# Routing stretch reordered, last two experts returned by one-hot products, final norm by rows

## The chip, the cores and the metric

The kernel runs on one core of one Trainium2 chip. The metric is the device time of one execution in microseconds. Five engines run their own instruction streams and meet at semaphores: TensorE (PE), VectorE (DVE), ScalarE (ACT), GpSimd (POOL) and SyncE (SP). POOL, SP and ACT also issue DMAs; those of SP carry the weights.

## The reference

One inference step of a two-layer backbone for 128 context tokens and 256 latent tokens, in float32, width 1024. What matters here is the second half of each layer and the final norm:

```
h2 = rmsnorm(x) * (1 + scale2) + shift2
x  = x + gate2 * moe(h2)            # 16 experts, 2 chosen for each token
...
y_prompt, y_sample = rmsnorm(xp, final_norm_g), rmsnorm(xs, final_norm_g)

def moe(h, ...):
    scores = sigmoid(h @ router_w); ...        # best group of 4, then its best 2 experts
    z = silu(h @ w_gate[e]) * (h @ w_up[e]) * gates[e]
    return sum over e of z @ w_down[e]         # w_gate, w_up: 1024x512, w_down: 512x1024
```

## The kernel before

All 384 tokens are three tiles of 128 rows (NT = 3; tile 0 is the context). The order of every engine's work is written out by hand; there is no scheduler. Each PSUM use is a job with a bank of its own (`place_jobs`), `fill`, `ready`, `release` and `moved` are the semaphore steps around it. A `step` waits until the instruction before it has written its result.

**Weights.** SP loads 2 MB blocks in the order `ISSUE` into six slots (`ring` 0 to 3, `extra` 4 and 5). A block is issued when the block that was in its slot has been read (`block_read`). Blocks are `ada` (modulation), `win`, `wout`, and for each expert gate, up and down. Beside the last products of layer 0, TensorE reads four `ada` blocks of layer 1, `AHEAD[0]`, by `mod_rows` (8 products each, 16 recorded instructions); `mod_turn` then turns their result.

**Routing stretch.** When x of a tile is done, it is normed, turned, modulated (`hidden_tile`), turned back and stored in DRAM as `hidden_rows` (ACT issues that store). `route` gives the logits; VectorE then runs some sixty small steps: scores, the one-hot choices `oh1`, `oh2`, each choice's place in its expert's list (`place6`), and, by a product with the one-hot `inplace`, the lists `lst` of at most 96 rows for each expert (CAP = 96). An expert with more rows than that would get a further round: the overflow table `ovt` holds their number and what they are. With these inputs there are none, and the overflow loop is only jumped over.

**Experts.** POOL gathers the 96 rows of an expert from `hidden_rows` into `xg` (L667), TensorE turns them (L1824) and runs gate, up and down (L1835), ACT and VectorE move the halves out of PSUM; the result lands in one of two buffers `ybuf` (VectorE L1414, L1416 last), and POOL scatters it to `expert_rows` in DRAM (L685), two rows for each token. The weights of expert e+1 land during expert e.

**End of a layer.** All five engines read `ovt` and jump over the overflow loop. POOL waits until every store has landed, reloads both rows of all tokens (L711, three DMAs of 1 MB, one for each tile), and VectorE adds them tile by tile, multiplies by the gate and adds to x (L1453 to L1455, 128x1024 each). ACT sums the squares (L733, L734), VectorE norms the tile (L1008 to L1003 small steps, L1010 the product). In layer 0 the first turns of layer 1 (L1510) follow, which wait for all three tiles. At the end of layer 1 one product with the final gain runs over all tiles (L1460), and SP stores the results.

## Time and profile before

| | |
|---|---|
| time of three runs | 1343.4, 1341.26, 1334.2 us, median 1341.26 |
| the profiled execution | 1344.76 us, its span 1343.1 us |
| TensorE busy | 1170.7 us, 87% of the span |
| VectorE, ScalarE, GpSimd busy | 525.6, 371.5, 249.6 us |
| chain that ended last | TensorE 74%, VectorE 14%, DMA 7% |
| layer 0: experts' products | 387.6 to 660.95 us |
| layer 1: experts' products | 1032.5 to 1305.9 us |

The span is from the first to the last recorded instruction. Within the experts TensorE has hardly a gap; outside them it often waits.

### The profile page before, as it was taken

The numbers are of one execution on the slowest core, as the hardware profiler recorded it, in microseconds if no ns is written. First come the engines' busy times: TensorE is split into PE (matmuls) and PEld (weight loads), VectorE is DVE, ScalarE is ACT, GpSimd is POOL, SyncE is SP. The second block draws the span as 40 slices with busy tenths as digits, with TensorE's granted clock in tenths as the row PEclk, the third lists the DMA queues.
The fourth block names the chain that finished last, engine by engine and source line by source line (L and its number), as shares of the span: only waits on it lengthen the run. The fifth ranks groups of instructions, "written<-read, shape, count | busy, mean of one in ns | idle before, by whom it ended". The sixth has DMA issues, their size and how long they took to land.

```text
span 1343.1 us, 19689 instructions
## 1 busy us (share of the span) xinstructions
PE 1170.7 (87%) x7740; PEld 540.9 (40%) x7740; DVE 525.6 (39%) x1276; ACT 371.5 (28%) x730; POOL 249.6 (19%) x361
## 2 busy tenths in 40 slices
PE   2899899789969999999629989988896999999980
PEld 0555555354423333333225655555443333333320
DVE  1274666733422111111154747575145111111125
ACT  2123344331312222222121424452222222222221
POOL 1221274220020111110020324440202011111000
PEclk9899889789879999999959997996996999999995
DMA  9738321555769999999380312064733999999924
GB/s 364 258 125 124 65 95 67 213 200 226 317 232 379 382 382 389 400 393 377 113 301 0 134 63 83 12 222 167 300 117 149 346 396 390 391 389 384 391 113 161
DMA packets 51488, 322.71 MB, mean 240 GB/s; under 512 B 8329, under 2 KB 8777, under 8 KB 32080
## 3 DMA queue, kind: packets, MB, share of 16 engines
q1 hardware_dynamic: 37552, 286.87, 55.3%
q0 software_dynamic: 12576, 30.03, 8.4%
q10 hardware_dynamic: 1280, 4.72, 0.9%
q8 instruction: 53, 0.87, 0.3%
q14 instruction: 27, 0.22, 0.1%
HBM read 315.53 MB, written 22.73 MB: 252 GB/s over the span
## 4 chain that ended last, share of the span: by engine, by line
PE 74%; DVE 14%; DMA 7%; issue 2%; ACT 2%; SPq 0%; DVEq 0%; POOLq 0%; ACTq 0%
PE ps L1835 38%; PE ps L1476 18%; PE ps L1724 6%; PE ps L1824 3%; DMA ring<-ada_w 3%; DVE attT L1103 3%; DVE dbuf L1082 2%; PE ps L1487 2%; PE ps L1510 2%; PE ps L1647 1%; PE ps L1618 1%; DMA ring<-w_out 1%; DVE small L1208 1%; DVE dbuf L1078 1%; DMA expert_rows<-big,lst 1%
## 5 line engine op out<-in xcount | busy, mean ns | idle before, releaser
L1835 PE MATMUL ps<-ring,dbuf 128*32 128x512 f32 x3072 | 390.2, 598 | 3.0 <-DVE dbuf L1395 1.6
L1835 PE MATMUL ps<-extra,dbuf 128*32 128x512 f32 x1536 | 198.4, 596 | 0.0
L1835 PEld LDWEIGHTS ps<-ring,dbuf 128*32 128x32 f32 x3072 | 108.6, 111 | 212.9 <-issue 207.4
L1476 PE MATMUL ps<-ring,extra 128*128 128x512 f32 (+1 forms) x384 | 149.8, 550 | 0.0
L1476 PE MATMUL ps<-extra,ring 128*128 128x384 f32 (+1 forms) x384 | 127.8, 481 | 7.6 <-ACT extra L763 5.1
L685 POOL DMA_INDIRECT expert_rows<-big,lst x32 | 30.0, 939 | 468.6 <-DVE big L1416 446.5
L1835 PEld LDWEIGHTS ps<-extra,dbuf 128*32 128x32 f32 x1536 | 56.1, 110 | 121.1 <-issue 120.9
L1476 PEld LDWEIGHTS ps<-ring,extra 128*128 128x128 f32 x384 | 74.0, 194 | 69.7 <-issue 66.2
L1476 PEld LDWEIGHTS ps<-extra,ring 128*128 128x128 f32 x384 | 75.7, 207 | 54.8 <-issue 12.7
L1395 DVE COPY dbuf<-ps 128x384 f32<-128x384 f32 x32 | 17.8, 558 | 200.5 <-PE ps L1824 200.4
L1724 PE MATMUL ps<-ring,extra 128*128 128x512 f32 x192 | 87.5, 612 | 7.6 <-DMA ring<-w_out 6.4
L952 ACT ACTIVATE big<-ps 96x512 f32<-96x512 f32 x32 | 19.0, 594 | 219.9 <-issue 163.1
L1487 PE MATMUL ps<-ring,scp 128*32 128x512 f32 x384 | 55.8, 717 | 26.9 <-DMA ring<-ada_w 26.9
L1405 DVE TENSOR_TENSOR big<-big,ps 64x512 f32<-64x512 f32 x32 | 21.7, 679 | 143.1 <-ACT big L961 143.1
L667 POOL DMA_INDIRECT dbuf<-hidden_rows,lst x32 | 31.2, 975 | 173.6 <-DMA hidden_rows<-big 75.8
L1414 DVE COPY big<-ps 64x512 f32<-64x512 f32 x32 | 22.2, 693 | 99.4 <-PE ps L1835 99.4
L1724 PEld LDWEIGHTS ps<-ring,extra 128*128 128x128 f32 x192 | 37.0, 197 | 51.5 <-issue 49.8
L1103 DVE COPY_PREDICATED attT<-mk,ps 128x128 f32<-128x128 uint16 x168 | 50.6, 301 | 15.6 <-PE ps L1647 10.0
L1510 PE MATMUL ps<-const,big 128*128 128x128 f32 x160 | 22.3, 287 | 35.5 <-DVE big L1010 35.5
L789 ACT ACTIVATE big<-ps 128x512 f32<-128x512 f32 (+2 forms) x42 | 21.6, 515 | 103.9 <-PE ps L1476 81.1
L467 POOL TENSOR_TENSOR dbuf<-bbuf 128x128 f32<-128x128 f32 x56 | 24.8, 443 | 132.6 <-PE ps L1647 128.9
L870 ACT ACTIVATE ring<-ps,small 128x384 f32<-128x384 f32 (+1 forms) x56 | 27.3, 488 | 71.8 <-DVE small L1209 71.0
(281 smaller groups left out, 1393.2 us busy)
## 6 DMA issues: line engine op xcount, KB each, us to landing
ring<-moe_w_up SPq DMA_DIRECT2D x30, 2048.0 KB, 14.1
ring<-ada_w SPq DMA_DIRECT2D x24, 2048.0 KB, 8.9
ring<-moe_w_gate SPq DMA_DIRECT2D x24, 2048.0 KB, 14.0
extra<-moe_w_down SPq DMA_DIRECT2D x22, 2048.0 KB, 14.4
ring<-w_in SPq DMA_DIRECT2D x12, 2048.0 KB, 11.6
ring<-moe_w_down SPq DMA_DIRECT2D x10, 2048.0 KB, 18.5
extra<-moe_w_gate SPq DMA_DIRECT2D x8, 2048.0 KB, 14.8
ring<-w_out SPq DMA_DIRECT2D x4, 2048.0 KB, 9.8
```

The costliest lines, as they stand in the source:

```text
L467: step(eng.tensor_tensor(strided(out, n * 2 * P + P + m, [-P, 2], [M, nb], [1, m]), right, ref, ALU.subtract))
L667: pool.indirect_dma_start(xg[0:CAP, e % 2, :], None, hrow, bass.IndirectOffsetOnAxis(lst[0:CAP, e, 0:1], 0), bounds_check=T - 1, oob_is_er ...
L685: pool.indirect_dma_start(yrow, bass.IndirectOffsetOnAxis(lst[0:CAP, e - 1, 1:2], 0), ybuf[0:CAP, (e - 1) % 2, :], None, bounds_check=2 * ...
L870: release(act, act.activation(prob[:, i % 2, mp, 0:nk], p[:, 0:nk], ACT.Exp, scale=scale, bias=nmx[:, i % 2, mp:mp + 1], accum_out=sums[:, ...
L1082: step(dve.tensor_tensor(o_, o_, strided(k0, 0, [HP * T + m, 2], [M, nb], [1, m]), ALU.mult))
L1103: ins = dve.copy_predicated(attT[:, 2 * u + h2, :], mk[:, 4 * g + k, :].bitcast(mybir.dt.uint16), p[:, k * P:(k + 1) * P])
L1476: ins = pe.matmul(out, a, b, start=(n == 0), stop=(n == len(pairs) - 1))
L1487: ins = pe.matmul(ps[c:c + 32, MOD_BANK, :], scp[:, 2 * b + k, :], w[:, 2048 * k + 512 * n:2048 * k + 512 * (n + 1)], start=(b == 0 and k ...
L1510: ins = pe.transpose(p[:, n * P:(n + 1) * P], s, ident)
L1724: ins = pe.matmul(p, hT[:, k, t * P:(t + 1) * P], w[:, k, :], start=(k == WO_ORDER[0]), stop=(k == WO_ORDER[-1]))
L1824: ins = pe.transpose(p[:, n * CAP:(n + 1) * CAP], s, ident[0:CAP, 0:CAP])
L1835: return pe.matmul(p[QT * g:QT * (g + 1), :], a, w, start=start, stop=stop, tile_position=(0, QT * g))
```

## The change

1. **Routing stretch, TensorE.** In layer 0 the four `ada` blocks of layer 1 are read at other places: none right after `route(0)`, the first after the first two products of the logits, the second behind `hidden_back(2)`, the last two together behind the lists.
2. **Routing stretch, VectorE.** The count of the overflow rounds is worked out before the lists (between `posn` and `lst`) and signalled by a semaphore of its own (`s_nov`). Behind the table come eight new steps: `yidx`, an index for each row of `expert_rows` that points out of bounds where the row's expert is 14 or 15 (and its place is under 96), and `late`, the one-hot matrices of those two experts' rows. The modulation of `AHEAD` stands behind them.
3. **Overflow loop in front.** Every engine reads the count and jumps before its first expert. SP holds the fourth expert block (`j == 3`) until the count is known and the first expert's rows have been gathered (`d_g[0]`); the third block goes to slot 5 in both layers.
4. **Last two experts.** Only experts 0 to 13 are scattered. In each layer POOL clears the two reload buffers during expert 4 (L731) and, as soon as the store of expert 13 has landed, fetches the others' rows by six indirect DMAs of 512 KB (L745). So that rows not yet written are finite, `expert_rows` is first filled with x by two DMAs (768 rows of 4 KB) on POOL's queue ahead of the skewed bias table (L627).
5. **The sum.** VectorE sums tile 0's fetched rows before it moves out the last half of expert 15, and tile 1's after; POOL does so for tile 2. TensorE multiplies `late` with `ybuf` (12 products with 512 columns), and `completed` adds the result times the gate to x.
6. **Norms.** They run tile by tile inside the sum; the final one takes the gain in the same instruction, and SP stores each tile by itself.

```diff
@@ SP, in the loop over ISSUE[l]
                     elif kind == "expert":
+                        if j == 3:
+                            overflow_weights(l)
+                            sp.wait_ge(d_g[0], 16 * (NE // 2 * l + 1))
@@ SP, at the end
-            sp.wait_ge(s_y, 1)
-            sp.dma_start(y_prompt[0], xn[:, 0, :]).then_inc(d_y, 16)
-            sp.dma_start(y_sample[0].rearrange("(t p) d -> p t d", p=P), xn[:, 1:3, :]).then_inc(d_y, 16)
+            for t in range(NT):
+                sp.wait_ge(s_y, t + 1)
+                sp.dma_start(y_sample[0, (t - 1) * P:t * P] if t else y_prompt[0], xn[:, t, :]).then_inc(d_y, 16)
@@ POOL
                 if l == 0:
+                    for rows_, src in ((yrow[0:2 * P], x_prompt[0]), (yrow[2 * P:2 * T], x_sample[0])):
+                        pool.dma_start(rows_.rearrange("(p k) d -> p k d", k=2),
+                                       src.unsqueeze(1).broadcast_to([src.shape[0], 2, D])).then_inc(d_init, 16)
                     pool.dma_start(skew, ...)
...
                 for b in range(2):
-                    pool.wait_ge(d_sc[b], 16 * (NE // 2) * (l + 1))
+                    pool.wait_ge(d_sc[b], 16 * ((NE - LATE) // 2) * (l + 1))
+                pool.wait_ge(s_late, l + 1)
                 for t in range(NT):
-                    pool.dma_start(yr[:, t, :, :], yrow[2 * t * P:2 * (t + 1) * P].rearrange("(p k) d -> p k d", k=2)).then_inc(d_yr[t], 16)
+                    for k in range(2):
+                        pool.indirect_dma_start(yr[k][:, t, :], None, yrow, bass.IndirectOffsetOnAxis(yidx[:, NT * k + t:NT * k + t + 1], 0),
+                                                bounds_check=2 * T - 1, oob_is_err=False).then_inc(d_yr[t], 16)
+                pool.wait_ge(d_yr[2], 32 * (l + 1))
+                y = yr[0][:, 2, :]
+                step(pool.tensor_tensor(y, y, yr[1][:, 2, :], ALU.add))
+                step(pool.tensor_tensor(y, y, gate[:, 1, :], ALU.mult))
+                pool.tensor_tensor(x[:, 2, :], x[:, 2, :], y, ALU.add).then_inc(s_sum2, 1)
@@ DVE, after the last expert but one
+                summed(0)
+                expert(NBODY, 0, last=True, next_=False)
+                summed(1)
+                completed(0)
+                completed(1)
+                normalize(2 * l + 2, 0)
+                dve.wait_ge(s_sum2, l + 1)
+                completed(2)
+                normalize(2 * l + 2, 1)
+                normalize(2 * l + 2, 2)
@@ DVE
+                def completed(t):
+                    for b in range(2):
+                        job = ("cm", l, t, b)
+                        p = ready(dve, job)
+                        tmp_ = dbuf[:, b * 512:(b + 1) * 512]
+                        release(dve, dve.tensor_tensor(tmp_, p, gate[:, min(t, 1), b * 512:(b + 1) * 512], ALU.mult), job)
+                        xs = x[:, t, b * 512:(b + 1) * 512]
+                        ins = dve.tensor_tensor(xs, xs, tmp_, ALU.add)
...
@@ PE, after expert 15
+                for t in range(NT):
+                    halves = [begin(pe, ("cm", l, t, b)) for b in range(2)]
+                    for j in range(LATE):
+                        if t == 0:
+                            for kind in ("dn0", "dn1"):
+                                moved(pe, (kind, l), NE - LATE + j)
+                        for b in range(2):
+                            ins = pe.matmul(halves[b], late[0:CAP, j, t, :], ybuf[0:CAP, j, b * 512:(b + 1) * 512], ...)
```

TensorE in the routing stretch of layer 0, before: `L1770` is `route`, `L1487` is `mod_rows`, `L1505` spreads the gates, `L1804` to `L1806` are the places and the last `L1476` the lists.

```order
178 L1770 MATMUL ps<-dbuf,wrt 32x256 x8
179 L1487 MATMUL ps<-ring,scp 32x512 x16
180 L1510 MATMUL ps<-const,big 128x128 x8
181 L1790 MATMUL ps<-const,dbuf 128x16 x2
182 L1487 MATMUL ps<-ring,scp 32x512 x8
183 L1770 MATMUL ps<-dbuf,wrt 32x128 x8
...
186 L1505 MATMUL ps<-bbuf,const 128x512 x4
...
191 L1476 MATMUL ps<-bbuf 96x48 x6
192 L1487 MATMUL ps<-ring,scp 32x512 x8
193 L1497 MATMUL ps<-const,dbuf 128x8 x4
194 L1824 MATMUL ps<-const,dbuf 128x96 x8
```

The same place after (`L1843` is `route`, `L1560` is `mod_rows`, `L1578` spreads the gates).

```order
178 L1843 MATMUL ps<-dbuf,wrt 32x256 x8
179 L1583 MATMUL ps<-const,big 128x128 x8
180 L1861 MATMUL ps<-const,dbuf 128x16 x2
181 L1560 MATMUL ps<-ring,scp 32x512 x8
182 L1843 MATMUL ps<-dbuf,wrt 32x128 x8
...
185 L1560 MATMUL ps<-ring,scp 32x512 x8
186 L1578 MATMUL ps<-bbuf,const 128x512 x4
...
191 L1549 MATMUL ps<-bbuf 96x48 x6
192 L1560 MATMUL ps<-ring,scp 32x512 x16
193 L1570 MATMUL ps<-const,dbuf 128x8 x4
194 L1967 TENSOR_LOAD ovt
...
196 L1968 COMPARE_AND_BRANCH
```

One block instead of three stands ahead of the second `route`, one ahead of the gates, two ahead of `mod_turn`, and the read of the count stands ahead of the first expert's turns.

VectorE between the places and the first expert, after (before, the rows 411 to 417 stood behind the lists, and the rows from 440 on did not exist, save the modulation 446).

```order
410 L1390 TENSOR_TENSOR attT<-ps,const 128x48
411 L1393 COPY attT<-ps 128x16
...
417 L1399 SCALAR_TENSOR_TENSOR attT<-const,attT 128x16
418 L1400 CAST ovt<-attT 1x1
419 L1402 TENSOR_SCALAR lst<-ps 96x16
...
439 L1429 CAST ovt<-attT 1x7
440 L1430 TENSOR_TENSOR attT<-attT 128x6
...
444 L1435 TENSOR_SCALAR attT<-lst 96x2 x3
445 L1436 TENSOR_TENSOR bbuf<-const,attT 96x768
446 L1063 TENSOR_TENSOR modv<-ps,par 128x32
447 L1472 TENSOR_LOAD ovt
...
464 L1447 COPY dbuf<-ps 128x384 x2
```

Eight small steps and one read of the count are added between the lists and row 464, which moves the first expert's turned rows, and eight small ones have left it.

VectorE at the end of layer 0, after: rows 540 and 545 are the last of experts 14 and 15, `L1500` to `L1502` are `summed`, `L1510` and `L1512` `completed`, `L1055` ends a norm.

```order
540 L1468 TENSOR_TENSOR big<-big,ps 64x512
541 L1500 TENSOR_TENSOR big<-big,bbuf 128x1024
...
543 L1502 TENSOR_TENSOR x<-x,big 128x1024
544 L1466 COPY big<-ps 64x512
545 L1468 TENSOR_TENSOR big<-big,ps 64x512
546 L1500 TENSOR_TENSOR big<-big,bbuf 128x1024
...
548 L1502 TENSOR_TENSOR x<-x,big 128x1024
549 L1510 TENSOR_TENSOR dbuf<-ps,gate 128x512
...
556 L1512 TENSOR_TENSOR x<-x,dbuf 128x512
...
562 L1055 TENSOR_SCALAR big<-x,small 128x1024
563 L1510 TENSOR_TENSOR dbuf<-ps,gate 128x512
...
578 L1055 TENSOR_SCALAR big<-x,small 128x1024
```

Before, nine products and sums of 128x1024 and then three norms stood here, all behind the reload.

## Rows read from the trace of the kernel before

**Rows 1.** Chain that ended last, end of layer 1: start us, us, what.

```profile
1300.55 5.39 PE ps L1835 x48
...
1308.28 3.41 DMA expert_rows<-big,lst
...
1312.27 5.08 DMA big<-expert_rows
...
1317.47 1.24 DVE big L1453
...
1334.08 3.36 DVE big L1460
```

**Rows 2.** The same chain, end of layer 0.

```profile
663.28 7.43 DMA expert_rows<-big,lst
...
693.27 2.83 PE ps L1510 x12
```

**Rows 3.** Timeline of VectorE: start us, us, line, operation, names, shapes.

```profile
661.75 0.68 DVE L1416 TENSOR_TENSOR big<-big,ps 64x512 f32<-64x512 f32 x1
...
687.97 0.15 DVE L1008 TENSOR_SCALAR small<-small 128x1 f32<-128x1 f32 x1
...
688.94 0.75 DVE L1010 TENSOR_SCALAR big<-x,small 128x1024 f32<-128x1024 f32 x1
...
1003.88 0.69 DVE L1063 TENSOR_TENSOR bbuf<-ps,gate 128x512 f32<-128x512 f32 x1 [4.54 <-PE ps L1724]
```

**Rows 4.** DMA issues, 1285 to 1343 us: size, median us to landing.

```profile
y_prompt<-big SPq DMA_DIRECT2D x1, 512.0 KB, 2.7
```

**Rows 5.** Chain, a `wout` product of layer 1 (8 products, 16 recorded).

```profile
996.90 6.88 PE ps L1724 x16
```

**Rows 6.** Window of the end of layer 1: us, busy us, granted clock, DMA share, GB/s.

```profile
1306.00:1312.00 6.00, 0.00 (x0) 0.00 (x0) 1.37 (x2) 0.00 (x0) 0.91 (x1) 0.88 0.10 29
```

**Rows 7.** Timeline of POOL: store of expert 13, layer 1.

```profile
1285.37 0.93 POOL L685 DMA_INDIRECT expert_rows<-big,lst  x1 [15.96 <-DVE big L1416]
```

**Rows 8.** Chain that ended last, routing stretch of layer 0.

```profile
364.24 10.27 DMA hidden_rows<-big
...
375.46 9.87 DMA dbuf<-hidden_rows,lst
...
387.60 9.43 PE ps L1835 x64
```

**Rows 9.** DMA issues, 1005 to 1045 us: the gathers in layer 1.

```profile
dbuf<-hidden_rows,lst POOLq DMA_INDIRECT x4, 4.1
```

**Rows 10.** Timeline of TensorE, routing stretch of layer 0.

```profile
350.21 3.62 PE L1487 MATMUL ps<-ring,scp 128*32 128x512 f32 x32
...
371.99 3.56 PE L1487 MATMUL ps<-ring,scp 128*32 128x512 f32 x16
376.45 1.03 PE L1497 MATMUL ps<-const,dbuf 128*128 128x8 f32 x8 [0.90 <-ACT dbuf L755]
```

**Rows 11.** Sources L1429 and L1904, reads of the count: ns min/median/max, starts.

```profile
L1429 DVEq TENSOR_LOAD <-ovt x2: 325/434/542, 662.5 to 1307.5; - x2
...
L1904 PEldq TENSOR_LOAD <-ovt x2: 860/884/909, 658.2 to 1303.1; - x2
```

**Rows 12.** Timeline of VectorE, routing stretch of layer 1.

```profile
1022.37 0.76 DVE L1341 TENSOR_TENSOR bbuf<-const,attT 128x576 f32<-128x576 f32 x1
...
1024.98 0.18 DVE L1348 TENSOR_SCALAR lst<-ps 96x16 uint32<-96x16 f32 x1 [1.74 <-PE ps L1476]
...
1031.86 0.56 DVE L1395 COPY dbuf<-ps 128x384 f32<-128x384 f32 x1
```

**Rows 13.** Source L604, the skewed bias table's writing in layer 0.

```profile
L604 POOL DMA_DIRECT2D skew_rows<-rpb_pad x1: 2827/2827/2827, 100.0 to 100.0; - x1
...
DMA to landing us min/median/max: 57.0/57.0/57.0
```

**Rows 14.** Timeline of POOL: the bias loads, which wait for it.

```profile
176.99 9.87 POOL L622 DMA_DIRECT2D extra<-skew_rows  x16 [0.33 <-POOL dbuf L475]
```

233 lines of the change are left out of this document (137 added, 96 removed).

## The prediction

> **What bounds the kernel now.** I read the profile's table first, then the chain that ended last, then the timelines at its joints. TensorE is busy for 87% of the span, and inside the experts it has no gap worth a change: this diff leaves those products alone. What it can move is the time in which TensorE waits for something else. There are four such places. At the end of layer 1 the last product ends at 1305.94 (1300.55 + 5.39) and the span at 1343.1: the last store takes 3.41, the reload of the first tile 5.08, and VectorE then works from 1317.47 to 1337.44 without a pause [rows 1]. The end of layer 0 is the same piece again, from the store at 663.28 (7.43 there) to the first turns of layer 1 at 693.27 [rows 2]. In the routing stretch of layer 0 TensorE waits for ACT's store of the hidden rows (10.27) and for POOL's gather (9.87), until the first expert's products start at 387.60 [rows 8]. In layer 1 a gather takes 4.1 [rows 9], and VectorE's chain of small steps, not the gather, is late: the copy at 1031.86 follows the table's last step directly [rows 12].
>
> **End of layer 1.** Today the last expert's rows leave VectorE at about 1307.44; in layer 0 the same instruction ends at 661.75 + 0.68 = 662.43 [rows 3]. What then stands on the path is store, reload, nine operations, three norms, one long product, two stores. In the changed kernel neither store nor reload stands there, if the fetched rows are there in time. Expert 13's store is issued at 1285.37 [rows 7]. Give it 3.4 as in [rows 1], or 7.4 as in [rows 2]: 1288.8 to 1292.8. Six fetches of 512 KB follow, one every 1.3 us (POOL issues an indirect DMA in 0.93 [rows 7] and needs some 0.35 between two), each landing 2.7 [rows 4] to 4.1 [rows 9] after its issue. Tile 0 is there by 1299, tile 2 by 1305. VectorE comes to tile 0 at about 1300.8, when expert 14 is moved out and TensorE has begun the last product of expert 15 [rows 1], and needs 3 x 1.26 = 3.8, up to 1304.6, before the last half of expert 15 at 1305.94. So the first sum is free; its cover is 1.4 us of VectorE's waiting, and any lateness of tile 0 beyond that is paid in full.
>
> From 1307.45 on VectorE is the bound: tile 1's sum 3 x 1.26 = 3.8 [rows 1]; `completed` for tiles 0 and 1, 8 operations of 128x512 at 0.69 and a gap, 0.73, so 5.8 [rows 3]; a norm, which is five small steps in 0.97 (687.97 to 688.94 [rows 3]) and one instruction with two inputs of 1024 that I price like L1453 at 1.3, so 2.3; `completed(2)` 2.9; two more norms 4.6. The sum is 19.4, so VectorE ends at 1326.9. The last tile's store lands 2.7 later [rows 4], and 0.4 remain to the span's end as now: 1330.0. **Gain 13.1.** ACT's squares for a tile lie beside VectorE's next operations, and POOL's three operations on tile 2 have 14 us.
>
> TensorE's twelve products lie beside this if they run at full clock. Eight products with 512 columns take 6.88 [rows 5], 0.86 each. They start at 1307.5, because their banks are those of `dn0` and `dn1`: tile 0 is complete at 1310.9, needed at 1311.2; tile 1 at 1314.4, needed in halves from 1314.2; tile 2 at 1317.8, needed at 1319.4. In the trace of before the granted clock has a mean of 0.88 in 1306 to 1312, with TensorE idle in all of it [rows 6]: it falls late, so the products begin at the full level. At the lower level from 1310.5 on, tile 2 would be complete at about 1323, and the gain smaller by up to 4.
>
> **End of layer 0.** The same steps start at 662.43: 3.8 + 5.8, a norm that ends in L1010 at 0.75 (1.76 with its small steps [rows 3]), `completed(2)` 2.9, two norms 3.5, together 17.8: the turns can start at 680.3 in place of 693.27 [rows 2]. **Gain 13.0.** Here the fetches are tighter: the weights of the last experts and the first block of layer 1 are still in flight, the store of expert 13 may take 7.4 as its later sister does [rows 2], and tile 0 comes at about 655.5, just as VectorE asks for it. I charge nothing and keep 3 us for the range. The remaining blocks of `w_in` are issued some 3 us before they are now and land before 680.
>
> **Routing stretch of layer 0.** SP no longer issues expert blocks 3, 4 and 5 before the first gather has landed. That takes the weights off the store and the gather: I give the gather its 4.1 of layer 1 [rows 9] in place of 9.87. The lists come about 0.5 us sooner, since one block's products stand ahead of the second `route` in place of three; but that `route` waits for tile 2's norm anyway, so the bounds are 0 and the 3.6 of the two blocks taken away [rows 10]. With the lists at 371.8 the gather lands at 376.8. Now TensorE is late: behind the lists stand two blocks. One took 3.56 there, two took 3.62 where the clock was full [rows 10], so two take between 3.6 and 7.1; I take 5.6, as the clock rises on the way. That gives 377.1; ACT's copy 0.9 and `mod_turn` 1.03 [rows 10] give 379.0. The read of the count takes TensorE 0.88 [rows 11], of which some 0.3 sticks out past `mod_turn`, with the branch 0.6: 379.6. From the turns to the products it takes 2.2 (375.46 + 9.87 to 387.60 [rows 8]): 381.8. **Gain 5.8**, bounds 3 and 10 (TensorE at the lower or the full level in this piece and in expert 0).
>
> The three held blocks need some 16 us once issued, so they are there by 394; expert 1 asks for the first of them some 20 us after 381.8. No cost.
>
> **Routing stretch of layer 1.** The first seven steps of the count move into VectorE's wait for the lists (1.74 [rows 12]), as does the count's copy: their eight small steps of 0.2 fill it, no gain and no loss there, and 1.75 less behind it. Added behind it are seven small steps, 1.4, and the 96x768 comparison, priced from the 128x576 one at 0.76 [rows 12] as 1.0: 2.4. So the copy of [rows 12] moves by +0.7. The read of the count stands ahead of it and is paid in full: 0.33 to 0.54 [rows 11], with register steps and branch an estimated 0.75. **Loss 1.4**, bounds 0.7 and 2.5. In layer 0 the same lies under TensorE's two blocks.
>
> **Filling `expert_rows`.** Two DMAs of together 3.1 MB stand on POOL's queue ahead of the skewed bias table, which is issued at 100.0 and lands 57.0 later [rows 13], while the bias loads ask for it at 176.99 [rows 14]: 20 us of cover. By the 512 KB store of 2.7 [rows 4] the filling takes 16 us; by the table's own bytes (3.8 MB in 57 us) 47 us. I take a value near the first, because its packets are 4 KB rows as in that store: nothing is paid. The other end costs 27 us.
>
> **POOL's two clears** in expert 4 and the wait for the filling lie in an interval in which POOL waits some 16 us for VectorE [rows 7]. No cost. The order in which three stores of y go out is in the first sum.
>
> **Sum.** 13.1 + 13.0 + 5.8 - 1.4 = 30.5 us. Against the profiled execution, 1344.76 - 30.5 = 1314.3. That execution was 3.5 above the median of the three runs, 1341.26, so for a median I forecast 1341.26 - 30.5 = 1311.
>
> **Rivals.**
> *The fetched rows are late* (12%). For it: in layer 0 they leave while weights land, and the gathers of [rows 8] took 9.87 in such company. Then VectorE stands at tile 0 while expert 15 waits behind it: 9.9 in place of 4 costs 4 to 6 us in layer 0, and with the clock's 4 us at one end: 1316 to 1321. Against it: SP is held by the same semaphores, so only what is already issued competes.
>
> *The jump over the loop costs more than the read* (10%). The skipped instructions stand ahead of the first expert, in front of both late engines, and if the target has to be fetched, it costs a DMA landing, 2.7 [rows 4], in each layer: +5.4, 1316. Against it: the loop of the experts jumps too, and TensorE has no gap there. The Trainium skill, Runtime: NRT & Kernel Launch, Instruction fetch mechanics, says that a taken branch whose target lies outside the two fetched pages forces a fetch before execution goes on; no row here shows such a stall.
>
> *The filling is slow* (5%, and the one that ends on the other side). If it runs at the table's rate, the table lands at 204 and POOL's exponents, which stand behind the bias, come 27 us late: 1338, no change. Each further microsecond is one more; from a filling of about 64 us on (1311 + 44 = 1355) the kernel would be over 1% slower. That takes a rate of 48 GB/s, under the table's own 67, so 3% for 1338 and 2% for slower.
>
> *The new order does not shorten the first stretch* (8%): TensorE at the lower level throughout and the lists no sooner, gain 3 in place of 5.8 and a loss of 2.5 in layer 1: 1315.
>
> **Chances and range.** The forecast's own case has 62% and reaches from 1304 (clock full, lists sooner) to 1317; the rivals above it 30% up to 1321; 3% lie below. One measurement of this kernel tells no change from one under 1% (13 us). The range 1303 to 1322 holds 8 in 10 and takes in the bounds of every unknown but the slow filling. Faster by over 1%, below 1328: 0.94; within: 0.04; slower: 0.02.
>
> **What would show it.** Right, if in the changed kernel the last turns' gap shrinks to some 18 us (660.95 to the turns), VectorE's last sum starts at once after expert 15, no store of experts 14 and 15 exists, and in layer 0 the hidden rows' gather lands in under 5 us. Wrong, if VectorE shows a wait for `expert_rows` ahead of the last half of expert 15, if `completed` waits for TensorE, if the bias loads start after 177, or if the first experts' products wait for a block.

## The result, and the profile after

The changed kernel takes 1329.77 us (median of 8 runs, 1325.59 to 1334.16), the kernel before 1338.95 in the same session (8 runs, 1334.2 to 1343.4). The ratio is 0.9936 with an interval of 0.9917 to 0.9956: some 9 us are gained, not the 30.5 that were forecast. In the profiled executions the span goes from 1343.1 to 1328.2 us, which is 14.9.

I cut both spans at the same places and set them against the terms of the prediction. The cuts are the end of the output projection, the first and the last expert product, and the first turn of the next layer.

| stretch | before, us | after, us | gain | forecast |
|---|---|---|---|---|
| up to the output projection's end, layer 0 | 348.5 | 345.0 | 3.5 | 0 |
| routing, layer 0 | 39.1 | 39.0 | 0.1 | 5.8 |
| experts, layer 0 | 273.4 | 276.3 | -3.0 | 0 |
| end of layer 0 | 32.3 | 21.4 | 10.9 | 13.0 |
| layer 1 up to its output projection's end | 310.5 | 306.7 | 3.8 | 0 |
| routing, layer 1 | 28.7 | 30.6 | -1.9 | -1.4 |
| experts, layer 1 | 273.5 | 283.2 | -9.8 | 0 |
| end of layer 1 | 37.2 | 26.0 | 11.2 | 13.1 |

The two gains of 3.5 and 3.8 are in stretches in which the change does nothing but the filling of `expert_rows`. In the profiles of the experiments below, which change nothing there, the first lies anywhere between 343 and 353 us and the second between 306 and 311. So I count them as chance: the other six stretches give 7.5 us together, which fits the medians' 9.2. Of the 23 us that are missing against the forecast's 30.5, 12.8 are in the two expert stretches, 6.2 in the routing stretches and 4.0 at the ends. In the table of the experiments below, the routing stretches start at SyncE's issue behind the projection and the expert stretches run to the start of the last product, so they differ from these by up to 0.7 us.

**The ends of the layers** are what the change was forecast to shorten, and they are shorter. The chain that ended last, of the changed kernel, has neither store nor reload between the last product and VectorE's work. First the end of layer 1, which answers to [rows 1], then layer 0, which answers to [rows 2]:

```profile
1295.29 6.92 PE ps L1908 x48
...
1303.73 1.51 DVE big L1500
...
1305.27 3.26 DVE big L1501
...
1308.55 1.24 DVE x L1502
...
1323.85 1.29 DVE big L1053
```

```profile
661.87 1.29 DVE big L1500
663.18 3.26 DVE big L1501
...
666.47 1.24 DVE x L1502
...
681.75 5.39 PE ps L1583 x24
```

One term in each sum is off: I priced the three steps of tile 1's sum at 1.26 each, and `L1501` takes 3.26 (in layer 1 `L1500` takes 1.51, too). GpSimd adds up tile 2 at that moment. Its timeline at the end of layer 0, and VectorE's beside it:

```profile
656.26 2.51 POOL L751 TENSOR_TENSOR big<-big,bbuf 128x1024 f32<-128x1024 f32 x1 [4.90 <-DMA bbuf<-expert_rows,attT]
658.85 3.21 POOL L752 TENSOR_TENSOR big<-big,gate 128x1024 f32<-128x1024 f32 x1
662.14 3.21 POOL L753 TENSOR_TENSOR x<-x,big 128x1024 f32<-128x1024 f32 x1
```

```profile
655.31 1.23 DVE L1501 TENSOR_TENSOR big<-big,gate 128x1024 f32<-128x1024 f32 x1
656.57 3.28 DVE L1502 TENSOR_TENSOR x<-x,big 128x1024 f32<-128x1024 f32 x1
...
663.18 3.25 DVE L1501 TENSOR_TENSOR big<-big,gate 128x1024 f32<-128x1024 f32 x1
666.47 1.23 DVE L1502 TENSOR_TENSOR x<-x,big 128x1024 f32<-128x1024 f32 x1
```

Twice a VectorE step that starts inside a GpSimd step ends 1.08 us behind that step's end: 659.85 against 658.77, and 666.43 against 665.35. By itself it takes 1.23. So it seems to wait for GpSimd and then to do nearly all of its work. The Trainium skill, SBUF — State Buffer, section "Who interferes with whom", says that a `tensor_tensor` with both inputs in SBUF contends with GpSimd's reads, and that the one that comes second waits for the other to finish. The rows agree with it, and e8 below takes GpSimd's steps away.

**The routing stretch of layer 0** should have lost 5.8 us and lost 0.1. (Three experiments that leave this stretch alone, e2, e8 and e12, have 37.2, 37.1 and 36.4 in their profiles where the changed kernel's has 38.5, so this one profile is a slow one by 1 to 2 us.) The timelines of TensorE, ScalarE, VectorE and SyncE's issues there, which answer to [rows 10]:

```profile
368.87 5.87 PE L1560 MATMUL ps<-ring,scp 128*32 128x512 f32 x32
378.19 1.85 PE L1570 MATMUL ps<-const,dbuf 128*128 128x8 f32 x8 [3.46 <-ACT dbuf L795]
379.89 1.52 PE L1897 MATMUL ps<-const,dbuf 96*128 96x96 f32 x8
```

```profile
377.45 0.60 ACT L795 ACTIVATE dbuf<-ps 128x512 f32<-128x512 f32 x1 [12.69 <-remote]
```

```profile
375.52 0.95 DVE L1436 TENSOR_TENSOR bbuf<-const,attT 96x768 f32<-96x768 f32 x1
381.82 0.19 DVE L1063 TENSOR_TENSOR modv<-ps,par 128x32 f32<-128x32 f32 x1 [5.34 <-remote]
383.41 0.56 DVE L1447 COPY dbuf<-ps 128x384 f32<-128x384 f32 x1 [1.40 <-issue]
```

```profile
374.40 0.34 SPq L559 DMA_DIRECT2D ring<-moe_w_up  x1
374.79 0.43 SPq L559 DMA_DIRECT2D ring<-moe_w_down  x1
377.36 0.33 SPq L559 DMA_DIRECT2D ring<-moe_w_gate  x1
```

The forecast's first half holds: SyncE issues block 3 at 374.40, as soon as the gather has landed, and GpSimd issued that gather at 370.16, so it took 4.2 us as forecast. The second half doesn't. By the records, whose ends are modelled, TensorE ends the two blocks at 374.74 and the small turn at 380.04. But ScalarE, which waits for the second block and nothing else, starts at 377.45. SyncE, which waits for the same product to free a slot, issues at 377.36. Both start within 0.1 us, so I take the product as complete at 377.35. In the same way VectorE's `L1063`, which waits for the small turn of 378.19, starts at 381.82. In the kernel before, the same turn of [rows 10] starts at 376.45 and the step that waits for it at 377.59, 1.1 us later. "remote" is the profile's way of saying that it found no releaser at that moment. A reader who trusts the ends of PE records sees nothing wrong there; the starts of those who wait show it.

**The expert stretches** were to be left alone. In layer 1 TensorE now waits for weights, which it never did before. Waits of TensorE in the changed kernel, 1018 to 1303 us (us in total, times, longest):

```profile
PE ps L1908 <- DMA ring<-moe_w_up: 5.5, 8, 1.3
PE ps L1908 <- ACT dbuf L996: 2.6, 1, 2.6
```

The second row is a single wait at expert 15, and layer 0 has its like (2.9), but no wait for weights. The starts of the experts' turns show the loss better: in the kernel before they follow each other by 16.9 us from the third expert on, in both layers. In the changed kernel layer 0 keeps that, and layer 1 has, from the seventh step on, 17.1, 17.4, 17.9, 18.0, 17.5, 18.5, 17.3, 18.3 and 17.5: 7.3 too many. With the 2.6 at expert 15 that is about the 9.8 of the table. Why the weights are late shows in SyncE's issues, first before and then after. Layer 1's products start at 1032 before and at 1019 after:

```profile
996.06 0.33 SPq L524 DMA_DIRECT2D ring<-moe_w_up  x1
1003.85 0.33 SPq L524 DMA_DIRECT2D extra<-moe_w_down  x1
1004.22 0.43 SPq L524 DMA_DIRECT2D ring<-moe_w_gate  x1
```

```profile
1015.16 0.33 SPq L559 DMA_DIRECT2D ring<-moe_w_up  x1
1015.54 0.43 SPq L559 DMA_DIRECT2D ring<-moe_w_down  x1
1016.01 0.43 SPq L559 DMA_DIRECT2D ring<-moe_w_gate  x1
```

And in windows of the changed kernel (us, busy us of TensorE, its weight loads, VectorE, ScalarE and GpSimd, granted clock, DMA share, GB/s): the DMA stands nearly idle from 1000 to 1015, and is then full (its share is 1.00 on the mean of 1030 to 1270).

```profile
1000.00:1015.00 15.00, 8.77 (x36) 5.28 (x34) 12.81 (x59) 4.87 (x7) 3.04 (x3) 0.73 0.14 48
1015.00:1030.00 15.00, 12.56 (x100) 4.63 (x104) 3.37 (x11) 2.85 (x4) 5.86 (x6) 0.77 0.91 308
```

**Smaller terms.** The first writing of `expert_rows` landed after 12.0 and 5.6 us. The skewed table behind it took 71.0 us in place of 57.0 and was there at 167.7, while the bias loads ask at 172.3: nothing was paid, as forecast. The jump over the overflow loop costs nothing that can be seen: in layer 1 VectorE goes from the end of the one-hot (1017.46) to the copy behind the jump (1018.37) in 0.91 us, with the read of the count in it. The prediction had 0.75 and, as a rival, 2.7 more in each layer. The Trainium skill, Runtime: NRT & Kernel Launch, section "Instruction fetch mechanics", says that a taken branch to a target outside the two fetched pages forces a fetch before execution goes on. No row here shows such a stall.

### The profile page after: what moved, and what is told of

The parts are those of the page before. It is cut to its first block, busy times and chain, and to the rows that moved or that the text cites. A ratio compares the mean times of both kernels' runs of the same rounds, so it can differ in the third digit from the quotient of the medians.

```text
span 1328.2 us, 19868 instructions
## 1 busy us (share of the span) xinstructions
PE 1194.4 (90%) x7788; PEld 550.4 (41%) x7788; DVE 545.4 (41%) x1309; ACT 374.1 (28%) x732; POOL 285.0 (21%) x375
## 4 chain that ended last, share of the span: by engine, by line
PE 68%; DVE 16%; DMA 11%; issue 2%; ACT 2%; another core or an unknown queue 1%; DVEq 0%; SPq 0%; ACTq 0%
PE ps L1908 31%; PE ps L1549 18%; DMA ring<-moe_w_up 7%; PE ps L1797 7%; PE ps L1897 3%; DVE attT L1148 3%; DVE dbuf L1127 2%; DMA ring<-ada_w 2%; PE ps L1583 2%; PE ps L1560 2%; PE ps L1691 1%; DVE small L1253 1%; PE ps L1720 1%; DMA ring<-w_out 1%
## 5 line engine op out<-in xcount | busy, mean ns | idle before, releaser
L1908 PE MATMUL ps<-ring,dbuf 128*32 128x512 f32 x3072 | 432.3, 601 | 12.1 <-ACT dbuf L996 5.5
L1908 PE MATMUL ps<-extra,dbuf 128*32 128x512 f32 x1536 | 209.6, 594 | 3.7 <-DMA ring<-moe_w_up 3.7
L1908 PEld LDWEIGHTS ps<-ring,dbuf 128*32 128x32 f32 x3072 | 118.4, 111 | 214.6 <-issue 203.6
L1549 PE MATMUL ps<-extra,ring 128*128 128x384 f32 (+1 forms) x384 | 121.2, 462 | 6.8 <-ACT extra L803 4.3
L737 POOL DMA_INDIRECT expert_rows<-big,lst x28 | 26.5, 946 | 421.9 <-DVE big L1468 421.9
L1908 PEld LDWEIGHTS ps<-extra,dbuf 128*32 128x32 f32 x1536 | 60.4, 110 | 134.0 <-issue 133.8
L1447 DVE COPY dbuf<-ps 128x384 f32<-128x384 f32 x32 | 17.8, 558 | 204.2 <-PE ps L1897 201.9
L1549 PEld LDWEIGHTS ps<-extra,ring 128*128 128x128 f32 x384 | 72.6, 198 | 50.8 <-issue 6.7
L992 ACT ACTIVATE big<-ps 96x512 f32<-96x512 f32 x32 | 19.0, 594 | 227.2 <-issue 169.0
L1560 PE MATMUL ps<-ring,scp 128*32 128x512 f32 x384 | 57.4, 735 | 23.6 <-DMA ring<-ada_w 23.6
L1797 PEld LDWEIGHTS ps<-ring,extra 128*128 128x128 f32 x192 | 37.4, 199 | 52.9 <-issue 51.2
L1005 ACT ACTIVATE big<-ps 96x512 f32<-96x512 f32 x32 | 19.0, 593 | 99.2 <-PE ps L1908 89.5
## 6 DMA issues: line engine op xcount, KB each, us to landing
ring<-moe_w_down SPq DMA_DIRECT2D x18, 2048.0 KB, 18.5
ring<-moe_w_gate SPq DMA_DIRECT2D x16, 2048.0 KB, 18.3
```

The source lines that it names most:

```text
L737: pool.indirect_dma_start(yrow, bass.IndirectOffsetOnAxis(lst[0:CAP, e - 1, 1:2], 0), ybuf[0:CAP, (e - 1) % 2, :], None, bounds_check=2 * ...
L1549: ins = pe.matmul(out, a, b, start=(n == 0), stop=(n == len(pairs) - 1))
L1560: ins = pe.matmul(ps[c:c + 32, MOD_BANK, :], scp[:, 2 * b + k, :], w[:, 2048 * k + 512 * n:2048 * k + 512 * (n + 1)], start=(b == 0 and k ...
L1797: ins = pe.matmul(p, hT[:, k, t * P:(t + 1) * P], w[:, k, :], start=(k == WO_ORDER[0]), stop=(k == WO_ORDER[-1]))
L1908: return pe.matmul(p[QT * g:QT * (g + 1), :], a, w, start=start, stop=stop, tile_position=(0, QT * g))
```

## The experiments

Each is the changed kernel with the edit shown, unless it says otherwise. "Interval" (95%) is that of the ratio to the kernel before, which had medians of 1338.5 to 1339.4 in these sessions. The stretches are from one profile each (us; experts to the start of their last products). In e4 the held blocks leave no cut at layer 1's projection:

| kernel | median | interval | routing 0 | experts 0 | end 0 | routing 1 | experts 1 | end 1 |
|---|---|---|---|---|---|---|---|---|
| before | 1339.0 | | 38.6 | 272.7 | 33.0 | 28.7 | 272.8 | 37.8 |
| changed | 1329.8 | 0.9917 to 0.9956 | 38.5 | 275.7 | 22.1 | 30.5 | 282.6 | 26.6 |
| e1 | 1329.1 | 0.9887 to 0.9944 | 37.2 | 275.9 | 22.7 | 36.1 | 276.2 | 26.2 |
| e2 | 1329.4 | 0.9890 to 0.9941 | 37.2 | 274.7 | 22.1 | 35.7 | 274.3 | 27.5 |
| e3 | 1322.5 | 0.9837 to 0.9916 | 37.2 | 275.3 | 22.4 | 30.6 | 272.4 | 27.5 |
| e4 (on before) | 1346.4 | 1.0030 to 1.0066 | 35.1 | 275.6 | 33.0 | | 279.4 | 37.8 |
| e5 | 1326.7 | 0.9885 to 0.9947 | 34.4 | 277.1 | 22.4 | 30.6 | 278.1 | 28.4 |
| e6 | 1325.5 | 0.9879 to 0.9944 | 30.7 | 277.8 | 22.9 | 30.5 | 278.2 | 26.7 |
| e7 | 1319.5 | 0.9819 to 0.9901 | 37.0 | 274.8 | 22.1 | 30.6 | 272.9 | 28.4 |
| e8 | 1335.1 | 0.9953 to 0.9996 | 37.1 | 275.8 | 25.2 | 30.5 | 281.5 | 28.0 |
| e9 | 1325.1 | 0.9869 to 0.9927 | 30.7 | 280.9 | 21.0 | 30.4 | 281.5 | 24.6 |
| e10 | 1318.3 | 0.9823 to 0.9891 | 32.1 | 273.4 | 22.5 | 30.3 | 275.7 | 26.4 |
| e11 | 1322.2 | 0.9836 to 0.9902 | 36.0 | 275.6 | 22.4 | 30.8 | 273.4 | 27.7 |
| e12 | 1338.6 | 0.9976 to 1.0017 | 36.4 | 272.1 | 30.4 | 30.4 | 277.7 | 34.3 |
| e13 (on before) | 1337.9 | 0.9975 to 1.0010 | 37.4 | 273.3 | 33.1 | 28.7 | 272.7 | 37.8 |
| e14 | 1329.0 | 0.9896 to 0.9943 | 32.0 | 277.6 | 24.1 | 30.3 | 282.2 | 26.8 |

**e1, no hold.** Theory: SyncE's new wait, which I had costed at nothing, starves the weight stream.

```diff
                         if j == 3:
                             overflow_weights(l)
-                            sp.wait_ge(d_g[0], 16 * (NE // 2 * l + 1))
```

> The changed kernel, in which SyncE no longer waits for the gathered rows of expert 0 before it issues weight block 3 of a layer; it still stands until the overflow count is known (about 5 us earlier than the gather lands, in both layers). Theory A, the hold starves the weight stream: layer 1's expert stretch (283.2 us, first product to last) gives back about 5 of its 9.8 us and layer 0's (276.3) some 1 to 3, while layer 0's gather lands up to 5 us later again behind the weights; in all 1321 to 1327. Theory B, the stream is slower for another reason (GpSimd's new work, the slot order, the rows returned): both stretches stay within 1 us of 283.2 and 276.3, and the time is 1330 or, by the later gather, 1333.

Layer 1's expert stretch gives back 6.4 us, as theory A said. But its routing stretch grows by 5.6, and the time stays. SyncE still stands until the count is known, and the count is known some 5 us before the gather lands: the three blocks go out from 0.6 us ahead of the gather to 0.3 behind it, and the turns that wait for it start 11.2 us after its issue, where the changed kernel has 4.0.

**e2, the hold in layer 0 only.**

```diff
-                            sp.wait_ge(d_g[0], 16 * (NE // 2 * l + 1))
+                            if l == 0:
+                                sp.wait_ge(d_g[0], 16 * (NE // 2 * l + 1))
```

> The changed kernel with that wait kept in layer 0 only. Theory A: layer 0 as in the changed kernel, layer 1's expert stretch about 278 instead of 283.2, time 1324 to 1326. Theory B: 1330 within 1.5.

The same picture: layer 1's experts take 274.3, its routing 35.7, nothing is gained. Both expected times were wrong, because I had left the gather of layer 1 out of them.

**e3, neither hold nor count.**

```diff
-                        if j == 3:
-                            overflow_weights(l)
-                            sp.wait_ge(d_g[0], 16 * (NE // 2 * l + 1))
```

> SyncE's part of the overflow loop and the wait for the gathered rows are both left out (the overflow loop's weights are never loaded; with these inputs no row overflows, so every computed value is the same). Blocks 3 to 5 of a layer go out as soon as their slots are free. Theory A: layer 1's expert stretch comes back to about 274 us, layer 0's to 273.5; layer 0's gather stands behind some 12 us of weights, which costs 3 to 6 us there; time 1318 to 1325. Theory B: 1330 or more, stretches unchanged.

Layer 1's experts take 272.4, and its routing stretch the same 30.6 as with the hold: 7.3 us faster than the changed kernel in the median. The experts' turns follow each other by 16.9 us throughout. SyncE issues at 991 to 992, before the last of the hidden rows is stored, so that weights and gather don't meet until the end. TensorE has no wait for a weight block in this kernel; it waits 7.0 for the gather, which is late, but no later than VectorE's one-hot.

**e4, the kernel before with the hold.**

```diff
                     elif kind == "expert":
+                        if j == 3:
+                            sp.wait_ge(d_g[0], 16 * (NE // 2 * l + 1))
```

> The kernel before, in which SyncE waits for the gathered rows of expert 0 before weight block 3 of each layer, and nothing else is changed. Theory A: layer 1's expert stretch grows from 273.5 to about 280 to 284 us and layer 0's by about 3, layer 0's gather lands some 5 us sooner; against the kernel before +4 to +9 us (1343 to 1348). Theory B: the expert stretches stay at 273.5 and the sooner gather is a gain, 1334 to 1339.

7.0 us slower than the kernel before in the same session, a ratio of 1.0048: layer 1's experts take 6.6 more, layer 0's 2.9 more, layer 0's routing 3.5 less. From the seventh step of layer 1 on the turns are 6.7 too far apart in all, with the same pattern as in the changed kernel. TensorE's waits in layer 1 now have the row that the changed kernel has:

```profile
PE ps L1837 <- DMA ring<-moe_w_up: 4.9, 6, 1.4
```

This settles the hold in layer 1 from both sides: it makes the loss where nothing else is changed, and without it the loss is gone. In layer 0 it costs only the kernel before: the changed one has no wait for a block there, and e3 leaves its 275.7 at 275.3.

**e5, the first modulation block early.** In the profile after, TensorE idles 3.1 us behind tile 0 and 1's `route`, its granted clock is 0.50 in the five microseconds that follow, and the block of modulation products that stood there before now stands ahead of the second `route`.

```diff
                 route(0, 0, 2 * P)
+                for blk in AHEAD[l][0:1]:
+                    mod_rows(*blk)
                 hidden_tile(2)
...
-                for blk in AHEAD[l][0:1]:
-                    mod_rows(*blk)
```

> The changed kernel with one thing in TensorE's order put back: the first block of the next layer's modulation products stands again ahead of the turns of tile 2's hidden rows, where TensorE is idle for 3.1 us in the profile after. Theory A (the new order left TensorE idle there, its clock fell to 0.50, and the block then stood ahead of the routing product of tile 2): the routing product starts 2 to 3 us sooner after the output projection's end, the lists are ready 2 to 3 us sooner, and layer 0's routing stretch takes 36 us or less instead of 38.5; time 1327 to 1328. Theory B (the expert products wait for the last two modulation blocks and the rows behind them, wherever the first one stands): the stretch stays at 38.5 within 0.7, 1330.

The routing stretch is 34.4, and the interval of the time overlaps the changed kernel's. The second `route` starts 7.7 us after the projection's end (351.16) in place of 10.5 (355.99). So "one block ahead in place of three" had not made the lists sooner, as the prediction thought: behind the idle time the granted clock was at its lower level (0.50 in 350 to 355; here, without the idle time, 0.97 in 348 to 353), and the one block then took 3.64 in front of the `route`.

**e6, no slot table.** Which work makes TensorE's completions late behind the lists?

```diff
-                for t in range(NT):
-                    for k in range(2):
-                        pool.indirect_dma_start(table, bass.IndirectOffsetOnAxis(slotu[:, t, k:k + 1], 0), pay[:, t, k, :],
-                                                None).then_inc(d_slot, 16)
```

> The changed kernel without GpSimd's twelve indirect stores of the slot table (the table is left out; only an overflowing row would read it, and none overflows here). Theory A (these stores are in the way of the two last modulation blocks: in the profile after, block two completes 4.8 us behind block one and the small turn behind it 3.5 us after its start, where 3.6 and 1.0 were expected): both delays go, ScalarE's copy of the modulation rows and VectorE's modulation come 3 to 5 us sooner, layer 0's routing stretch takes 34 to 36 us, time 1326. Theory B (something else holds TensorE up there): VectorE's modulation still stands 5.3 us behind its one-hot, stretch 38.5, time 1329 to 1330.

Theory A, and by more than it gave: 30.7. The median of 1325.5 is where theory A had it, though its interval overlaps the changed kernel's. VectorE's modulation follows the one-hot at once, and the product starts at 373.5:

```profile
370.54 0.95 DVE L1431 TENSOR_TENSOR bbuf<-const,attT 96x768 f32<-96x768 f32 x1
371.53 0.19 DVE L1058 TENSOR_TENSOR modv<-ps,par 128x32 f32<-128x32 f32 x1
```

**e7, as e3, with block 2 of layer 1 in slot 1.**

```diff
-EXPERT_SLOTS = [[3, 4, 5, 1, 2, 0], [3, 4, 5, 1, 2, 0]]
+EXPERT_SLOTS = [[3, 4, 5, 1, 2, 0], [3, 4, 1, 2, 5, 0]]
```

> As e3_no_hold_no_count (SyncE's part of the overflow loop left out, no wait for the gathered rows), and block 2 of layer 1 goes to slot 1 as in the kernel before, so that it needn't wait for the output projection. Theory A (more weights ahead of the gather are worth more): layer 1's expert stretch stays at 272.4, its routing stretch 28.7 to 30.6; time 1321 to 1323, no more than 1 us better than e3, since 272.4 is already what TensorE needs. Rival: the block lands during the output projection and slows it, 1324.

1319.5 against 1322.5; the intervals overlap, and no stretch of the two differs by more than 1. The order of the slots isn't shown to matter once the stream is free.

**e8, tile 2 on VectorE.**

```diff
-                step(pool.tensor_tensor(y, y, yr[1][:, 2, :], ALU.add))
-                step(pool.tensor_tensor(y, y, gate[:, 1, :], ALU.mult))
-                pool.tensor_tensor(x[:, 2, :], x[:, 2, :], y, ALU.add).then_inc(s_sum2, 1)
...
-                dve.wait_ge(s_sum2, l + 1)
+                summed(2)
```

> The changed kernel in which VectorE instead of GpSimd adds up tile 2's two rows, behind tile 0's normalization. Theory A (the two engines slow each other: in the profile after, the product by the gate takes VectorE 3.25 us instead of 1.23 while GpSimd works on tile 2): that instruction is back at 1.23 us in both layers, 2.0 us each, and tile 2's three operations cost VectorE 3.7 us each time, so the ends of the layers take 1 to 2 us more each; 1331 to 1333. Theory B (it waits on something else): it stays at 3.25 us and the time is 1335 or more.

The cause is as theory A said: the product by the gate takes 1224 to 1226 ns all six times, where in the changed kernel two of its four took 3.25. Which of GpSimd's accesses is in the way isn't tested.

```profile
L1496 DVE TENSOR_TENSOR big<-big,gate x6: 1224/1224/1226, 653.4 to 1318.0; 128x1024 f32<-128x1024 f32 x6
```

The time is 5.4 us worse than the changed kernel's, more than I had worked out; the ends explain 4.5 of it. So GpSimd's help seems worth having in spite of what it costs VectorE, though the intervals just overlap.

**e9, the table only on overflow.** The six stores of each layer move:

```diff
                 with pool.If(n_ov > 0):
                     pool.wait_ge(s_ovt, l + 1)
+                    for t in range(NT):
+                        for k in range(2):
+                            pool.indirect_dma_start(table, bass.IndirectOffsetOnAxis(slotu[:, t, k:k + 1], 0), pay[:, t, k, :],
+                                                    None).then_inc(d_slot[l], 16)
```

> The changed kernel with the slot table's twelve indirect stores moved into the branch that runs only if a row overflows (none does here), so that nothing is left out. Theory A (the stores hold up TensorE's completions behind the routing): as e6_no_slot_table, layer 0's routing stretch 30 to 32 us instead of 38.5; of that some 2 us are given back in the expert stretch behind it, where the weights now come sooner than they can be supplied; time 1323 to 1326. Theory B (e6 was a lucky profile, the stores cost nothing): 1329 to 1330.

Routing 30.7 again, now with nothing left out. The median is 1325.1, and its interval, too, overlaps the changed kernel's. But the experts of layer 0 take 5.2 us more than in the changed kernel. Some 2.5 of them are starvation: the last five steps between the turns take 17.1 to 17.8 in place of 16.9. Products that start sooner use up sooner what lead there is. Another 1.3 are expert 0's products, at a granted clock of 0.86 in their first 20 us in place of 0.92. So in part the stores hid what the hold costs.

**e10, the table on overflow, and the weights early.** As e9; blocks 3 to 5 go out when their slots are free, and an overflow loads them again behind its loop:

```diff
-                        if j == 3:
-                            overflow_weights(l)
-                            sp.wait_ge(d_g[0], 16 * (NE // 2 * l + 1))
+                        if j == ESLOTS:
+                            overflow_weights(l)
```

> As e9, and blocks 3 to 5 of a layer go out as soon as their slots are free; an overflow reloads them after its loop; block 2 of layer 1 in slot 1 again. So nothing is left out and nothing holds the stream. Theory A (hold and stores are the two losses of the change, independent of each other): layer 1's expert stretch 272.5, layer 0's routing stretch 31 to 34 (the gather lands behind weights again), time 1313 to 1318. Theory B (the stores only hurt where the held weights start at the same moment): no better than e7_no_hold_old_slots, 1319 to 1320.

1318.3: 11.5 us under the changed kernel and 20.5 under the kernel before, with nothing left out. In time it can't be told from e7 (1319.5). In the profile the two losses are both small: routing 32.1 in layer 0, experts 273.4 and 275.7, of which 2.7 are the wait at expert 15.

**e11, and the modulation block early.** The edits of e10 and of e5 together.

> As e10, with the first modulation block ahead of the turns of tile 2's hidden rows as in e5_ada_product_early. If what that gave there (3 us in the median) adds up: 1310 to 1316, and under e10 by 1 to 3 us. If TensorE then waits for the gathered rows anyway: the same as e10 within 1 us.

Not faster (1322.2; the intervals overlap). The profile has the reason, in SyncE's and TensorE's rows:

```profile
368.56 0.34 SPq L564 DMA_DIRECT2D ring<-moe_w_down  x1
```

```profile
379.86 1.54 PE L1900 MATMUL ps<-const,dbuf 96*128 96x96 f32 x8 [6.54 <-DMA dbuf<-hidden_rows,lst]
```

TensorE is at full clock, ends the next modulation block sooner and frees its slot at 368.5; a weight block of 2 MB starts in that microsecond, the gather is issued at 368.19 and lands beside it after 11.6 us. In e10 the same block left at 372.94, 2.4 us behind the gather, and the turns started 6.7 us after the gather's issue (377.24 against 370.57). And the gather of expert 1, issued 1.0 us ahead of that block (371.92), took 10.2. Neither kernel has a store of the table here. GpSimd's gathers of e11, from issue to landing:

```profile
DMA to landing us min/median/max: 4.0/11.6/15.8
```

**e12, the reload late.**

```diff
+                moved(pool, ("zt", l), NE - 1)
                 pool.wait_ge(s_late, l + 1)
                 for t in range(NT):
```

> The changed kernel in which GpSimd asks for the rows in memory only after the last expert's product has been turned and read (about 7 us later). In the profile after, expert 15 of layer 0 takes 2.7 us more than before: TensorE's and ScalarE's steps there come late while the six reloads run. Theory A (the reloads cause that, as the slot table's stores do behind the routing): layer 0's expert stretch is back at 273, and the end of the layer takes some 3 to 5 us more, since rows 0 and 1 arrive later; 1332 to 1338. Theory B (it is the code behind the loop or the weights): the stretch stays at 275.7.

Theory A: the expert stretch of layer 0 is back at 272.1. Layer 1's falls too, from 282.6 to 277.7, and its single wait at expert 15 is gone, while it still waits for weights (4.3 in all). ScalarE in expert 15, first in the changed kernel, where GpSimd issues the six fetches from 643.76 to 651.4, then in e12:

```profile
644.74 0.59 ACT L1001 ACTIVATE big<-ps 64x512 f32<-64x512 f32 x1 [2.51 <-PE ps L1908]
649.61 0.59 ACT L1005 ACTIVATE big<-ps 96x512 f32<-96x512 f32 x1 [4.28 <-remote]
...
652.68 0.49 ACT L996 ACTIVATE dbuf<-ps 128x384 f32<-128x384 f32 x1 [1.87 <-remote]
```

```profile
645.17 0.59 ACT L1002 ACTIVATE big<-ps 64x512 f32<-64x512 f32 x1 [2.52 <-PE ps L1909]
648.54 0.59 ACT L1006 ACTIVATE big<-ps 96x512 f32<-96x512 f32 x1 [2.78 <-PE ps L1909]
...
650.94 0.49 ACT L997 ACTIVATE dbuf<-ps 128x384 f32<-128x384 f32 x1 [1.20 <-PE ps L1898]
```

From the same step 7.94 us pass in the one and 5.77 in the other, 2.2 of the 3.6 that the stretches differ by. The ends grow by 8 us each, so the early reload is right, and its price is some 3 us in each layer.

**e13, the kernel before without the table's stores.**

```diff
-                        pool.indirect_dma_start(table, bass.IndirectOffsetOnAxis(slotu[:, t, k:k + 1], 0), pay[:, t, k, :],
-                                                None).then_inc(d_slot, 16)
```

> The kernel before without the slot table's indirect stores (the table is left out; only an overflowing row would read it, and none does). Theory A (the change moved the waits of TensorE, ScalarE and VectorE into the stretch of the stores, the kernel before had only the gather there): its gather landing of 9.9 us is what weights in front of it cost, and stays; layer 0's routing stretch 37.5 to 38.6, time 1336 to 1339. Theory B (the stores slow whatever is in flight, the gather too): the gather lands in 4 to 6 us, the routing stretch is 33 to 35 us, and the time 1332 to 1335.

Neither theory by itself. The gather lands 4.2 us after its issue at 373.18, where in [rows 8] it took 9.87. But that isn't the stores' absence: the gather of expert 1 (374.52) takes 11.1 without them. What differs is the next weight block. It is issued 1.9 us behind the first gather and 0.6 behind the second; in the kernel before it stands 0.16 behind the first (375.62 against 375.46). The gathers of e13:

```profile
DMA to landing us min/median/max: 4.2/7.0/11.1
```

The product starts at 383.80, 1.3 us sooner as counted from the projection. VectorE does its overflow table up to 383.15 and then the copy, and that was hidden behind the gather, so a sooner gather gains little in this kernel:

```profile
377.64 1.52 PE L1820 MATMUL ps<-const,dbuf 96*128 96x96 f32 x8
```

**e14, the stores one expert later.**

```diff
+                    if e == 1:
+                        for t in range(NT):
+                            for k in range(2):
+                                pool.indirect_dma_start(table, bass.IndirectOffsetOnAxis(slotu[:, t, k:k + 1], 0), pay[:, t, k, :],
+                                                        None).then_inc(d_slot, 16)
```

> The changed kernel with the slot table's stores issued behind the gather of expert 3, beside the products of experts 0 and 1, instead of ahead of them (an overflow would then find no table; none occurs here). Theory A (they hurt only where a short chain of completions hangs on the stretch): layer 0's routing stretch 30.7 as in e9, the expert stretch no longer than in e9 (280.9 in its profile); time 1325 to 1327. Theory B (they delay completions wherever they run): the routing stretch is 30.7, but the expert stretch grows by 3 to 5 us more in each layer, and the time is 1330 or more.

The routing stretch is 32.0 and the experts' are not clearly longer than e9's (277.6 and 282.2 against 280.9 and 281.5), which speaks for theory A. But in layer 1 the step between the turns beside which the stores now stand takes 13.2 in place of 11.8, and the time of 1329.0 isn't the 1325 to 1327 that theory A asked for; e9's 1325.1 can't be told from either. I leave it undecided.

## Why the prediction was wrong

**The ends of the layers: right, each 2 us too large.** 11.2 and 10.9 in place of 13.1 and 13.0. The rows came back in time and VectorE found them there, TensorE's long products stayed ahead of it, and in layer 0 `completed` followed the last sum at once. The term that was mis-sized is "tile 1's sum 3 x 1.26": it measured 1.51 + 3.26 + 1.24 = 6.0 in layer 1 and 1.29 + 3.26 + 1.24 = 5.8 in layer 0. The prediction said that GpSimd's three operations "have 14 us", and asked only if they would be ready, not what they do to VectorE meanwhile. e8 shows that GpSimd's steps were the cause.

**"The three held blocks need some 16 us once issued ... No cost": the step that failed.** It cost some 7 us in layer 1: 7.3 by the steps between the turns, 6.6 where nothing else differs (e4), 7.3 in the median when it is left out (e3). In layer 0 it cost the changed kernel nothing that its waits show.

I had asked when the first held block would be wanted, and it was there. I should have asked how long the stream can do without its lead. An expert takes TensorE 273.5 / 16 = 17.1 us, and in that time asks for three blocks of 2.1 MB, and for a gather and a store of 96 rows of 4 KB: 7.1 MB. The DMA moved 385 to 398 GB/s when it was full, 6.7 MB in 17.1 us. So each expert uses up an estimated 0.4 MB of the lead, 6 to 7 MB over a layer. The kernel before had its whole lead of six blocks, 12.6 MB, when the products began: its DMA share is 0.29 and 0.22 in the two 15 us from 1015 to 1045, because all slots are full and SyncE issues nothing between 1004.22 and 1042.10. Then the share is 1.00 from 1045 to 1270, and the prediction nowhere uses it. The change begins its products at 1019 with the three blocks only just under way, an estimated 12 us or 5 MB poorer, and runs dry from expert 6 on: the first wait for a block is at 1133.70.

A block's time from issue to landing shows it coming. For a gate block it is 10.7 us at the start of layer 1 before (issued 1053.34) and 17.4 at its end (1256.11), and no product waits. In the changed kernel it is 16.3 at 1055.70 and 20.8 at 1106.39, and it stays near 21 while TensorE waits. The byte count alone would let the stream run longer (12.6 less 5 MB are more than 6 to 7 MB); a block can only be asked for when its slot has been read, so not all of the lead can be used up. That last step is my reading; the landing times are what the profiles show. A transfer that is moved later costs nothing only if the queue behind it has slack to the end.

**Routing of layer 0, "Gain 5.8": right about the gather, wrong about what comes after.** The gather fell from 9.87 to 4.2 us, and putting the 9.87 down to weights fits the runs: gathers with a weight block issued within 1.2 us took 9.4 to 15.8, with the stores (before) and without (e10, e11, e13). But I looked at what stands before the gather and not at what GpSimd issues behind it. The slot table's stores then took the gain: TensorE's two blocks needed 8.5 us (368.87 to 377.35) in place of my 5.6, and the turn behind them 3.6 in place of 1.03. Take the stores away and the stretch falls to 30.7 (e6, e9), 2.1 below my forecast, which is 38.6 - 5.8 = 32.8 by the cuts of that table. A smaller part is the clock: I let it "rise on the way", and took its lower level as a bound, but did not see that the new order itself makes the idle time behind which it is low (e5).

**The reload beside expert 15.** 3 us in layer 0 and 2.6 in layer 1, 0 forecast. The reload made this (e12), not the filling or the clears. I had weighed whether the fetches would be late, never whether they would make others late.

**Routing of layer 1: 1.9 lost, 1.4 forecast.** From the lists to the copy it was 6.88 before and is 8.31 now, 1.43 more, as worked out. The other half microsecond lies ahead of the lists.

**The rivals** all moved the forecast by single terms; none of them took the hold. The signs of being wrong had it, "if the first experts' products wait for a block", but only the first experts': the first wait came in expert 6. The rival that comes nearest, "the fetched rows are late", names the right collision of row fetches with others' work, but on the wrong side. The range ended 8 us below the result because three steps that I had set at nothing had no bounds at all.

## What to carry to other kernels

If the DMA share is 1.00 through a stage, holding its queue back before the stage eats lead, and once the lead is gone it is paid inside the stage, however early the first block is there: compare bytes asked per step with bytes moved, and price the hold by the lead it eats. A DMA of many small rows must be priced for what it does to those beside it, in a stretch where a short chain of completions decides. And two edits that each gain can meet: what a faster engine frees is issued at once, here within 0.4 us of the gather (e11), so the pair has to be read together.

## What the runs showed of the hardware

Six indirect stores of 128 short rows each, issued 1.3 us apart, held up things that have nothing to do with them: a product's completion reached two other engines 2.6 us after the modelled end, and a small turn's 1.7 us after. Row fetches of 512 KB did a milder form of it. That these DMAs are the cause is shown (e6, e9, e12); by which path they reach TensorE, whether its instruction supply, the delivery of completions or its operands, is not, since the records of TensorE have modelled ends. In e4 the turn started at 375.93, the first of the stores was issued at 376.06, and the turn was still done in 1.1 us: a store did not hurt there in its first microsecond. How long after its issue it begins to, stays open.

A gather of 96 rows from GpSimd landed in 3.8 to 4.6 us where the next 2 MB block was issued 1.9 us behind it or later, or long before it (layer 1 of before; e6, e9, e10, e13), and in 9.4 to 15.8 where a block was issued between 1.2 us ahead and 1.0 behind (layer 0 of before, e10, e11 and e13). Each of these gaps is what the kernels happened to have; none was set on purpose.

VectorE's sum or product of two 128x1024 tiles, 1.23 us alone, took 3.25 to 3.35 where it started inside such a step of GpSimd, and GpSimd's steps took 2.4 to 3.2.
